# Differential-attention outputs kept undivided under their norm, and two of four map pairs mixed on GpSimd

## The reference

```python
def diff_alibi_mixer(qc, kc, vc, ..., subln, lam_init, pos):
    ...
        logits = jnp.einsum('bqhid,bshid->bhiqs', qb, k).astype(f32) * scale
        bias = -slopes[:, None, None, None] * jnp.abs(qp[:, None] - pos[None, :])[None, None]
        p = jax.nn.softmax(logits + bias, axis=-1)
        a = (p[:, :, 0] - lam * p[:, :, 1]).astype(v.dtype)
        return jnp.einsum('bhqs,bshe->bqhe', a, v)
    o = from_blocks(lax.map(block, (to_blocks(q), pos.reshape(S // Q_BLOCK, Q_BLOCK))))
    o = rmsnorm(o, subln) * (1.0 - lam_init)
```

## Time and profile before

| what | value |
|---|---|
| median of three runs | 2961.04 us |
| the profiled execution | 2959.69 us |
| its span | 2957.8 us, mean granted clock 0.992 |
| PE busy | 2869.4 us (97%) |
| DVE busy | 1990.9 us (67%) |
| ACT busy | 1317.6 us (45%) |
| POOL busy | 463.3 us (16%) |
| chain that ended last | PE 83%, DVE 9%, issue 4%, ACT 3% |

### The profile page before, as it was taken

How to read it: one execution, slowest core, us unless ns; L and a number is a source line. 1 busy time by engine, 2 the same in 40 slices (tenths; PEclk the granted TensorE clock), 3 DMA queues, 4 the chain that set the end, 5 groups by cost and what they waited for, 6 DMA issues and landing times.

```text
span 2957.8 us, 36854 instructions
## 1 busy us (share of the span) xinstructions
PE 2869.4 (97%) x13552; PEld 2278.2 (77%) x13552; DVE 1990.9 (67%) x2316; ACT 1317.6 (45%) x1844; POOL 463.3 (16%) x243
## 2 busy tenths in 40 slices
PE   7999889999999999999999998899999999999998
PEld 6777646888888888888877785478788888888887
DVE  3987888982465565556678788889716555565555
ACT  4327888993322222222333288889724122212223
POOL 1211332233300000000131123322341000000002
PEclk9999999999999999999999999999999999999999
DMA  5455332432221111111135543234312121112102
GB/s 199 155 169 128 88 82 60 103 103 58 57 59 56 43 43 56 43 43 43 42 134 203 167 97 72 64 87 107 99 46 69 43 58 43 43 43 66 47 29 57
DMA packets 236532, 236.67 MB, mean 80 GB/s; under 512 B 59520, under 2 KB 199680, under 8 KB 236416
## 3 DMA queue, kind: packets, MB, share of 16 engines
q1 hardware_dynamic: 236416, 235.13, 28.1%
HBM read 184.24 MB, written 50.86 MB: 79 GB/s over the span
## 4 chain that ended last, share of the span: by engine, by line
PE 83%; DVE 9%; issue 4%; ACT 3%; DMA 1%; SPq 0%; POOL 0%; ACTq 0%; DVEq 0%
PE ps L1826 31%; PE ps L1841 16%; PE ps L1563 11%; PE ps L1665 9%; PE ps L1737 5%; PE ps L1703 4%; PE ps L1704 3%; PE ps L1699 2%; DVE ps L1263 2%; PE ps L1806 1%; DVE r L1248 1%; PE ps L1750 1%; PE ps L1594 1%; DVE r L1285 0%; DVE r L1291 0%
## 5 line engine op out<-in xcount | busy, mean ns | idle before, releaser
L1665 PE MATMUL ps<-stack 128*128 128x512 f32 (+1 forms) x1152 | 346.3, 418 | 44.7 <-ACT prob L935 19.0
L1461 DVE TENSOR_TENSOR xT<-ps,xT 128x512 f32<-128x512 f32 x352 | 241.5, 690 | 210.1 <-PE ps L1841 209.9
L1665 PEld LDWEIGHTS ps<-stack 128*128 128x128 f32 (+1 forms) x1152 | 206.9, 191 | 159.2 <-ACT prob L935 51.4
L1737 PEld LDWEIGHTS ps<-ident_r,prob_r 128*128 128x128 f32 x2048 | 231.8, 142 | 100.0 <-issue 23.5
L935 ACT ACTIVATE prob<-ps,nmx 128x1024 f32<-128x1024 f32 x256 | 285.2, 1114 | 20.2 <-PE ps L1737 10.0
L1426 DVE SCALAR_TENSOR_TENSOR cv<-u,vec,cv 128x1024 f32<-128x1024 f32 x176 | 225.8, 1283 | 89.0 <-ACT cv L1076 78.7
L1088 ACT ACTIVATE ah<-cv 128x1024 fp32r<-128x1024 f32 x44 | 46.7, 1061 | 528.8 <-DVE cv L1439 528.8
L1371 DVE TENSOR_TENSOR ptl<-ps,pth 128x512 fp32r<-128x512 f32 x384 | 256.3, 684 | 37.4 <-ACT pth L997 33.6
L1826 PE MATMUL ps<-xgh,w0h 128*128 128x512 f32 x704 | 274.7, 390 | 0.0
L1826 PE MATMUL ps<-xgl,w0h 128*128 128x512 f32 x704 | 273.9, 389 | 0.0
L1826 PE MATMUL ps<-xgh,w0l 128*128 128x512 f32 x704 | 273.9, 389 | 0.0
(11 more groups left out here) (253 smaller groups left out, 5571.6 us busy)
## 6 DMA issues: line engine op xcount, KB each, us to landing
wraw<-in_w_up SPq DMA_DIRECT2D x88, 512.0 KB, 5.0
draw<-in_w_down SPq DMA_DIRECT2D x22, 1024.0 KB, 5.0
stack<-ka_d SPq DMA_DIRECT2D x64, 256.0 KB, 5.6
wraw<-in_w_in SPq DMA_DIRECT2D x30, 512.0 KB, 4.2
vst<-v_d SPq DMA_DIRECT2D x48, 256.0 KB, 3.8
x_d<-xT SPq DMA_DIRECT2D x2, 4096.0 KB, 17.6
wraw<-in_w_out SPq DMA_DIRECT2D x16, 512.0 KB, 5.2
stack<-qc_d SPq DMA_DIRECT2D x64, 128.0 KB, 3.6
```

Of the source, the lines that this page charges most:

```text
L1461: ins = dve.tensor_tensor(xs, ps[:, 4 + j % 4, :], xs, ALU.add)
L1665: ins = pe.matmul(score_banks(i)[:, kh, :], st[q][0:rows, c0:c0 + P], st[k][0:rows, kh * HALF:(kh + 1) * HALF], start=n == 0, stop=n == le ...
L1737: ins = pe.transpose(ps[:, 4 + s % 2, m * P:(m + 1) * P].bitcast(F32R), prob_r[:, b, m, s * P:(s + 1) * P], ident_r[:, :])
```

## The change

Group C's outputs are no longer divided by the sum s of the first map. DVE copies a unit's output from PSUM to `xg_plain`, a plain float32 view laid over `xgh`; the inverse of the sums, its four transposes on PE, the copy to `nrm`, the rounding on ACT and the subtraction on POOL are gone for C units, and so is `sum_c`. The first maps' sums are kept in `csum` for the whole layer. POOL works eps s^2 (times the head's width) out of them, in `floor_c`, and PE adds it to the sums of squares with one matmul of 32 columns. And `POOL_MIXES` is `(0, 1)`: pair 1 is mixed on POOL too, and DVE has pairs 2 and 3 left.

```diff
-POOL_MIXES = (0,)
+POOL_MIXES = (0, 1)
...
+        plain = ExitStack()
+        xg_plain = sb(plain, "xg_plain", [P, KT, T])
+        plain.close()
         xgh, xgl = sb(ctx, "xgh", [P, KT, T], F32R), sb(ctx, "xgl", [P, KT, T], F32R)
...
+        def sum_column(x, q):
+
+            return 2 * (x["h"] // 2 * TT + x["half"] * 4 + q) + x["h"] % 2
...
                 def lo_mix(x):
                     rows = slice(HD * x["par"], HD * x["par"] + HD)
-                    pool.wait_ge(mix_hi, l * NU + x["u"] + 1)
+                    if x["group"] == "C":
+                        return
+                    pool.wait_ge(mix_hi, l * NAB + x["ab"] + 1)
...
-                def sum_c():
-
-                    for c in range(2):
-                        pool.tensor_tensor(prob1a[:, c, :], xgh[:, 6 + c, :].bitcast(F32), xgl[:, 6 + c, :].bitcast(F32), ALU.add).then_inc(c_summed, 1)
+                def floor_c():
+
+                    pool.wait_ge(c_out, (l + 1) * 2 * NC)
+                    settle(pool)
+                    pool.tensor_scalar(cfloor[:, :], csum[:, :], cst[:, C_EPS + 1:C_EPS + 2], None, ALU.mult).then_inc(c_floor_half, 1)
+                    pool.wait_ge(c_floor_half, l + 1)
+                    pool.tensor_tensor(cfloor[:, :], cfloor[:, :], csum[:, :], ALU.mult).then_inc(c_floor, 1)
...
                 def copy_norm(x):
 
-                    act.wait_ge(norm_done, l * NU + x["u"] + 1)
-                    act.wait_ge(o_ready, l * NU + x["u"] + O_CREDIT)
+                    if x["group"] == "C":
+                        return
...
                     if x["group"] == "C":
                         dve.wait_ge(av_done, l * (8 * NU) + x["u"] * 8 + 8 + AV_CREDIT)
-                        dve.wait_ge(norm_copied, l * NU + x["u"] + 1 + N_CREDIT)
-                        dve.wait_ge(mix_lo, l * NU + x["u"] + MIX_CREDIT)
-                        dve.tensor_tensor(osum[rows, :], ps[rows, 6 + x["half"], :], nrm[rows, :], ALU.mult).then_inc(o_ready, 1)
+                        dve.tensor_copy(mix_at(xg_plain, x), ps[rows, 6 + x["half"], :]).then_inc(c_out, 1)
                         return
...
+                    if c == 0:
+                        pe.wait_ge(c_floor, l + 1)
+                        pe.matmul(ps[:, 2, 0:4 * TT], ident, cfloor[:, :], start=True, stop=False)
                     pe.wait_ge(c_squared, l * 2 + c + 1)
...
-                        if s == 6:
-                            pe.wait_ge(dinv_done, l * NU + x["u"] + 1)
+                        if s == 6 and x["group"] != "C":
+                            pe.wait_ge(dinv_done, l * NAB + x["ab"] + 1)
```

More of the change, by code:

```diff
@@ L720, in mix_maps @@
                     pool.wait_ge(mixed_first, n)
-                def sum_c():
-                    for c in range(2):
-                        pool.tensor_tensor(prob1a[:, c, :], xgh[:, 6 + c, :].bitcast(F32), xgl[:, 6 + c, :].bitcast(F32), ALU.add).then_inc(c_summed, 1)
+                def floor_c():
[4 more added lines that the diff above has]
+                    pool.tensor_tensor(cfloor[:, :], cfloor[:, :], csum[:, :], ALU.mult).then_inc(c_floor, 1)
                 def pool_unit(x, prev, nx, after):
                     if x["k"] == NU - 2:
-                        sum_c()
+                        floor_c()
                     second = nx and nx["group"] == "C"
@@ L982, in hi_mix @@
                 def hi_mix(x):
-                    act.wait_ge(o_ready, l * NU + x["u"] + 1 + O_CREDIT)
+                    if x["group"] == "C":
+                        return
+                    act.wait_ge(o_ready, l * NAB + x["ab"] + 1 + O_CREDIT)
                     rows = slice(HD * x["par"], HD * x["par"] + HD)
@@ L1339, in reciprocal_sums @@
                     b = x["half"]
-                    sums = rsum[:, b, 0:8:2] if x["group"] == "C" else rsum[:, b, 0:4]
+                    if x["group"] == "C":
+                        return
                     dve.wait_ge(exp_done, l * NS + x["item0"] + x["items"] + EXP_CREDIT)
                     if x["k"]:
-                        dve.wait_ge(norm_done, l * NU + x["u"])
-                    dve.reciprocal(dinv[:, 0:4], sums).then_inc(dinv_done, 1)
+                        dve.wait_ge(norm_done, l * NAB + x["ab"])
+                    dve.reciprocal(dinv[:, 0:4], rsum[:, b, 0:4]).then_inc(dinv_done, 1)
                 def sum_output(x):
@@ L1371, in dve_unit @@
                             dve.tensor_tensor(ptl[:, s % NPT, :], ps[:, 4 + s % 2, :], pth[:, s % NPT, :].bitcast(F32), ALU.subtract).then_inc(pt_lo, 1)
-                        if s == (1 if x["group"] == "C" else 0):
+                        if s == 0:
                             reciprocal_sums(x)
@@ L1382, in scale_c @@
                     dve.wait_ge(c_spread, l * 2 + c + 1)
-                    dve.scalar_tensor_tensor(two(prob1b[:, c, :]), two(prob1a[:, c, :]), small[:, 5:6], ps[:, 2 * c:2 * c + 2, :],
+                    dve.scalar_tensor_tensor(two(prob1b[:, c, :]), two(xg_plain[:, 6 + c, :]), small[:, 5:6], ps[:, 2 * c:2 * c + 2, :],
                                              ALU.mult, ALU.mult).then_inc(c_normed, 1)
@@ L1692, in value_product @@
                     if s == 0:
-                        pe.wait_ge(norm_copied, l * NU + x["u"] + N_CREDIT)
+                        if U_C < x["k"] <= U_A:
+                            if x["k"] < U_C + 2:
+                                pe.wait_ge(o_read, l * NAB + x["u"] - 1 + O_CREDIT)
+                            else:
+                                pe.wait_ge(c_out, l * (2 * NC) + x["u"] - 1 - U_C)
+                        else:
+                            pe.wait_ge(norm_copied, l * NAB + x["ab"] + N_CREDIT)
+                            if x["k"] == U_A + 1:
+                                pe.wait_ge(c_out, (l + 1) * (2 * NC))
                         if x["half"] == 0:
@@ L1710, in sum_squares_c @@
                         o = 2 * (c * TT + m)
-                        ins = pe.matmul(ps[:, 2, o:o + 2], prob1b[:, c, m * P:(m + 1) * P], blk[:, 0:P:HD], start=True, stop=True)
+                        ins = pe.matmul(ps[:, 2, o:o + 2], prob1b[:, c, m * P:(m + 1) * P], blk[:, 0:P:HD], start=False, stop=c == 1 and m == TT - 1)
                     ins.then_inc(c_stat, 1)
```

37 lines of the change are left out of this document (21 added, 16 removed).

## The result

| kernel | median | runs | ratio to before (95%) |
|---|---|---|---|
| before | 2963.21 us (2960.94 to 2966.09) | 4 | |
| after the change | 2996.74 us (2994.20 to 2999.61) | 4 | 1.012 (1.0108 to 1.0132) |

The change costs 1.2%, 33.5 us by the medians, where + 21.3 had been forecast; the time is 2.7 us beyond the range's upper end. The profiled execution took 2999.61 us, with a span of 2997.1 us and a mean clock of 0.979; before it was 2957.8 us and 0.992, so the two traces lie 39.3 us apart. Units 8 to 14 of the two layers, counted from first transposes to first transposes, hold 39.2 of it, 19.6 in each layer; what the traces differ in elsewhere cancels.

What follows compares the result with a forecast made beforehand. Group C's units were taken as bound by a loop of dependences, no engine full. Profiled 2959.69 + 17.9 (hold) + 3.4 (clock) = 2981.0, median 2982.3 us; own range 2973 to 2994, 8-in-10 range 2958 to 2994.

Steps and rivals of the forecast that it cites:

- + 0.2 for unit 7: Unit 7, transposes of B and mixes of C: mix of pair 2 starts 0.2 us later per layer.
- - 0.25 for unit 15: Unit 15, bound by PE: 0.4 us saved on transposes of inverses, 0.15 added by the new matmul, per layer.
- "DVE's order" and the loop without mix 1: DVE at a C unit's end: without pair 1's mix, maximum 0 starts earlier and the loop gains 0.54 us a unit.
- "The two engines hold each other up.": Group C: DVE's mix of pair 2 waits until 0.20 us before POOL's second addition ends, starting 1.35 us later.
- "Mix 2 starts 10.48 us after POOL begins mix 0.": C units: the delay from POOL starting pair 0 to DVE's mix of pair 2 is 10.48 us, or more.
- "I take 1.7; it is the same engine reading SBUF": Unit 14: POOL's scaling holds DVE's mix as an addition does, + 1.7 us; without that hold + 0.8.
- "+ 17.9 us": Both layers: the unit terms of the loss, 8.9 us per layer, before any effect of TensorE's clock.
- "I take half: + 3.4 us in all.": TensorE's clock falling at unit starts: 0.49 us on scores, up to 3.4 us a layer, half taken, + 3.4 in all.
- "stays low for two or more steps in every unit": Rival: TensorE's clock falls and stays low, up to + 1.3 us a unit, 2997 us; chance 0.06.
- "the stretch there had B's steps around it": Argument against a long-lasting low clock: the earlier trace's granted 0.64, at unit 8's start, lay among group B's steps.
- rivals without a hold: Rival: POOL's second mix runs freely beside DVE's mixes, gaining 10.3 us in all, 2950.8 us; chance 0.08.
- with POOL alone held: Rival: DVE goes on while POOL's mix of pair 1 stands still; 2961 us, give or take 3; chance 0.10.

Runs made afterwards that it cites:

- 4th experiment: Changed kernel plus 7 spare matmuls of 512 columns on PE before it waits for the mixes of a group C unit: 2982.39 us, ratio 1.0066 to before.
- third experiment: Changed kernel with POOL's second addition (pair 1) replaced by a scaling by 1, leaving out pair 1's second-map product: 2969.18 us, ratio 1.0024 to before.
- seventh experiment: Undivided outputs, POOL mixing pair 0 alone, plus 5 spare matmuls in each of PE's two waits at unit 8's start: 2954.42 us, ratio 0.9980 to before.
- first experiment: Changed kernel with POOL mixing pair 0 alone again, outputs of group C still undivided: 2958.55 us, ratio 0.9988 to before.
- tenth experiment: Changed kernel with a scaling for POOL's second addition, plus 4 spare matmuls before each group C unit's wait for mixes: 2957.26 us, ratio 0.9996 to before.
- the fifth: Changed kernel with pair 1 divided by columns, POOL mixing 384 of 1024 and DVE the other 640: 2951.95 us, ratio 0.9974 to before.

## Why the prediction was wrong in size and right in kind

The direction, the place and the mechanism stood as forecast; the price of TensorE's clock did not. By unit, the time from one unit's first transposes to the next one's, over the kernel before, in layer 0:

| unit | forecast | hold alone (4th experiment) | changed kernel |
|---|---|---|---|
| 8 | + 1.34 | + 1.99 | + 1.97 |
| 9 | + 1.35 | + 1.51 | + 3.42 |
| 10 | + 1.35 | + 1.47 | + 1.98 |
| 11 | + 0.95 | + 1.22 | + 3.85 |
| 12 | + 0.95 | + 1.22 | + 1.70 |
| 13 | + 1.35 | + 1.48 | + 3.77 |
| 14 | + 1.7 | + 0.98 | + 2.92 |
| sum | + 9.0 | + 9.9 | + 19.6 |

Layer 1 has + 19.6 in the changed kernel too. The forecast's other two terms, + 0.2 for unit 7 and - 0.25 for unit 15, measured + 0.51 and - 0.44 in layer 0.

- **"DVE's order" and the loop without mix 1.** Right: maximum 0 started 0.91 us after its score (392.02 - 391.11; the forecast had 0.92), the mix of pair 2 1.66 after that (1.68).
- **"The two engines hold each other up."** Right: mixes of 3.0 to 3.2 us, pair 3 at 1.28 in units 9 to 13, POOL's scalings and additions unstretched. In unit 8 pair 3 was to be 1.28 as well and took 1.78: the subtraction for a B output, which stays, was left out of the sum, and the 0.50 us are most of that unit's 1.97 against 1.34.
- **"Mix 2 starts 10.48 us after POOL begins mix 0."** A little short. With the clock kept up POOL began mix 0 at 384.65 and the hold ended at 395.29 (393.23 + 3.34 - 1.28), 10.64 later: between two mixes POOL paused 0.23 us, not the 0.08 that lies between the two halves of one. That is 0.16 us a unit and most of what is left in units 9, 10 and 13.
- **Unit 14, "I take 1.7; it is the same engine reading SBUF".** Wrong: the other value, + 0.8, was the right one (+ 0.98 measured). The scaling did not hold the mix that came 1.61 us after its start. The Trainium skill, page "SBUF — State Buffer", section "Who interferes with whom", had both halves of this rule: the two-input DVE instruction contends with any GpSimd instruction that reads SBUF, which the 0.83 us of the third experiment agrees with, and the pair is kept for the whole instruction, which the additions agree with (2.16 of 2.36 us) and the scaling contradicts (0.83 of 2.77). The error is small, 0.7 us a layer, and to the other side.
- **The sum "+ 17.9 us".** Right within the measurement: 19.5 us (14.8 to 24.3) remained with the spare matmuls. It helped that two errors cancel, unit 8 too low by 0.65 and unit 14 too high by 0.7.
- **"I take half: + 3.4 us in all."** This is the step that failed, a term of the sum sized too small. The clock cost 16 us or more by the fourth experiment, 9.7 a layer by the table. The price was taken from a single score, 0.49 us. What the clock slows is whole steps of scores, transposes and value products: 3.41 us instead of 2.96 for the first, 3.15 instead of 1.69 for the second, and some tenths of a third. By the table, columns three and four, that is 0.5 us in a unit with the short dip and 1.9 to 2.6 in one with the long dip, and it fell in every unit from 8 to 14. The dip in the earlier trace rows already held slow steps of that kind (the first two of unit 8 took 3.41 and 2.30 us in the kernel before, and 2.96 and 1.74 with the dip filled in the seventh experiment), and the prediction read only one row of it.
- **The rival "stays low for two or more steps in every unit", 2997 us at 0.06.** It came out to the microsecond, and that is partly luck: its "up to + 1.3 us a unit" is near the mean of what the clock cost in units 8 to 14 (9.7 / 7 = 1.4), but the units had 0, 0.5 or 1.9 to 2.6, with two slow steps in four of the six units 9 to 14 and not in every one. The argument that held it down, "the stretch there had B's steps around it", did not hold: the fourth experiment only filled the wait, and the dips of units 9 to 14 went, in layer 1 but for two. The wait itself (about 3 us, which the forecast had) should have weighed more, since a wait of that kind was in the trace with the dip right behind it.
- **Undivided outputs, "- 0.25" a layer.** The first experiment gives 0.9 to 5.9 us for both layers, 3.6 in the middle, more than the 0.5 forecast. In its trace unit 15 is 0.47 and 0.43 us shorter in the two layers. The rest can't be placed: outside of group C the same stretch differs by more than that from trace to trace (units 0 to 7 of layer 0 take 110.3 to 116.3 us over the twelve traces).
- **The rivals without a hold or with POOL alone held.** Excluded by the 3 us mixes.

What stays open: why some dips are long and some short. Nothing in these traces distinguishes the unit in front of a long dip from that in front of a short one, and no run was made for it.

## What to carry to other kernels

Moving work to an idle engine is only worth the time in which both engines can run: here a two-input addition on GpSimd and a two-input mix on VectorE, both in SBUF, excluded each other, so look at which of the two will be in flight when the other becomes ready, and size the moved piece to end before (with the undivided outputs, 384 or 512 of 1024 columns made the kernel 0.3% faster, and all of them made it 1.2% slower). When a change lengthens a wait of TensorE that already had a fallen clock behind it somewhere in the trace, price the fall by the whole steps behind that place, not by one instruction. And a few spare matmuls in such a wait are a cheap test of how much of a loss is clock.

## What the runs showed of the hardware

- A mix (scalar_tensor_tensor, two SBUF inputs) beside a GpSimd addition or subtraction of two SBUF tiles starts moving 0.20 us before that operation's recorded end, for 1024 columns (2.36 us), for 512 (1.29 us) and for 64 x 512 (1.58 us, unit 8 of the changed kernel) alike.
- Beside a GpSimd scaling by a constant (one SBUF input, 2.77 us) it is held for the first 0.83 us only, in all 16 units of the third experiment, where it came 0.08 to 0.47 us after the start. A scaling by a per-partition factor let a mix through that came 1.61 us after its start; its first 0.8 us were not tried with DVE in second place.
- With DVE in front, the scaling is the one that waits: 3.56 instead of 2.77 us for 1024 columns in the tenth experiment, and 1.56 for 384 columns in the fifth, of which some 1.1 are its own (an estimate from the end of VectorE's part: no such scaling ran free).
- A wait of 2.5 to 3.3 us in TensorE was followed by a fallen granted clock in each of the units 8 to 14, in both layers of the changed kernel, and waits of 1.2 to 1.5 us in some (group C at 0.94 in the third experiment). Filled with 7 matmuls of 512 columns (1.79 us), the same waits left it up at the start of 10 of the 12 units 9 to 14 of both layers.
